# Two-block transformer layer on one core: the second layer's feed-forward part moved into the program of its attention

## The reference, cut to what matters

```python
ya = _dilated_attention(qa, ka, va)                     # width 512
yb = _mla(c_q, c_kv, k_r, ...)                          # width 512
y = concat([rmsnorm(ya, out_norm_a), rmsnorm(yb, out_norm_b)]) @ w_o
x = x + rmsnorm(y, norm_mix_post)
h = rmsnorm(x, norm_ffn_pre)
u = dwconv(h @ w_up, conv_w, conv_b)                    # 3 taps along the tokens, 2 x 2816 columns
g, v = u[..., :D_FF], u[..., D_FF:]                     # D_FF = 2816
y = (gelu(g, approximate=True) * v) @ w_down
x = x + rmsnorm(y, norm_ffn_post)
# rmsnorm(x, g) = x * rsqrt(mean(x*x) + EPS) * g
```

## Time and profile before

| | us |
|---|---|
| median of 3 runs | 2170.84 (2170.11 to 2176.09) |
| profiled execution, its own time | 2173.72 |
| its span, first to last instruction | 2171.1 |
| PE busy | 1936.4 (89%) |
| second attention's last output product ends | 1906.1 |
| first `downs` product starts | 1939.9 |
| the last unit's `downs` starts | 2150.9 |

### The profile page before, as it was taken

How to read it: one execution, slowest core, us unless ns; L and a number is a source line. 1 busy time by engine, 2 the same in 40 slices (tenths; PEclk the granted TensorE clock), 3 DMA queues, 4 the chain that set the end, 5 groups by cost and what they waited for, 6 DMA issues and landing times. The chain is left out here.

```text
span 2171.1 us, 24938 instructions
## 1 busy us (share of the span) xinstructions
PE 1936.4 (89%) x9338; PEld 1049.2 (48%) x9340; DVE 622.1 (29%) x1362; ACT 434.6 (20%) x855; POOL 67.3 (3%) x86
## 2 busy tenths in 40 slices
PE   5999797998989979999898888989989888979997
PEld 2436353886878543333333333233333245657774
DVE  2376346245520121111111111111111123442223
ACT  2122550326231011111111110111111022411011
POOL 1000310100000000000000000000000000000000
PEclk9999898798999989999999999999999999989998
DMA  9443336214374469999999999999999872034442
GB/s 348 144 167 137 131 98 145 94 55 143 93 282 164 161 248 418 418 418 417 417 417 418 418 417 419 418 419 418 416 418 417 336 267 78 1 118 153 162 148 87
DMA packets 150651, 566.73 MB, mean 261 GB/s; under 512 B 35872, under 2 KB 43808, under 8 KB 112736
## 3 DMA queue, kind: packets, MB, share of 16 engines
q1 hardware_dynamic: 150592, 565.92, 67.2%
HBM read 555.26 MB, written 10.62 MB: 261 GB/s over the span
## 5 line engine op out<-in xcount | busy, mean ns | idle before, releaser
L2006 PE MATMUL expert_gb<-expert_ring,hT 128*64 128x512 f32 x1024 | 270.4, 607 | 69.6 <-DMA expert_ring<-in_w_gu 68.1
L2006 PE MATMUL expert_lb<-expert_ring,hT 128*64 128x512 f32 x1024 | 262.8, 592 | 0.0
L1911 DVE TENSOR_SCALAR hT<-expert_gb 128x512 f32<-128x512 f32 x32 | 22.1, 692 | 717.0 <-PE expert_lb L2006 717.0
L2054 PE MATMUL expert_yb<-expert_ring,hT 128*64 128x512 f32 x512 | 222.7, 592 | 1.5 <-DMA expert_ring<-in_w_down 1.4
L2054 PE MATMUL expert_yb<-expert_ring,h2T 128*64 128x512 f32 x512 | 222.8, 592 | 0.0
L2006 PEld LDWEIGHTS expert_gb<-expert_ring,hT 128*64 128x64 f32 x1024 | 59.4, 135 | 250.2 <-DMA expert_ring<-in_w_gu 200.5
L446 PE MATMUL mix_in_pj<-hT,mix_in_pj_ring 128*128 128x512 f32 (+1 forms) x384 | 147.1, 542 | 4.0 <-DVE hT L567 4.0
L2006 PEld LDWEIGHTS expert_lb<-expert_ring,hT 128*64 128x64 f32 x1024 | 72.8, 137 | 147.0 <-issue 147.0
L2711 PE MATMUL ffn_pu<-ffn_hT,ffn_wu 128*128 128x256 f32 x640 | 141.4, 379 | 0.0
L2054 PEld LDWEIGHTS expert_yb<-expert_ring,hT 128*64 128x64 f32 x512 | 69.9, 137 | 143.3 <-issue 140.5
L2711 PEld LDWEIGHTS ffn_pu<-ffn_hT,ffn_wu 128*128 128x128 f32 x640 | 121.6, 190 | 25.1 <-issue 9.6
(11 more groups left out here) (474 smaller groups left out, 2288.1 us busy)
## 6 DMA issues: line engine op xcount, KB each, us to landing
expert_ring<-in_w_gu SPq DMA_DIRECT2D x256, 1024.0 KB, 19.7
expert_ring<-in_w_down SPq DMA_DIRECT2D x128, 1024.0 KB, 20.7
fill_w<-in_w_fill SPq DMA_DIRECT2D x48, 512.0 KB, 3.7
mix_in_wm<-in_w_mod SPq DMA_DIRECT2D x11, 2048.0 KB, 9.1
ffn_wu<-in_w_up_units SPq DMA_DIRECT2D x22, 1024.0 KB, 6.2
mix_in_pj_ring<-in_w_in_units SPq DMA_DIRECT2D x12, 1024.0 KB, 4.8
ffn_wd<-in_w_down SPq DMA_DIRECT2D x22, 512.0 KB, 3.4
expert_ring<-in_w_in SPq DMA_DIRECT2D x4, 2048.0 KB, 11.4
```

Of the source, the lines that this page charges most:

```text
L1911: v.tensor_scalar(glu, gb[j][:], LIMIT, None, ALU.min).then_inc(s_glu, 1)
L2006: m = pe.matmul(b[halves[h], :], xT[:, k, x], ring[:, z, c0 + 512 * h:c0 + 512 * h + 512], start=False, stop=(k == KT - 1))
L2054: m = pe.matmul(yb[h][halves[j], :], hidT[j][:, c, hh * SLOTS:(hh + 1) * SLOTS], ring[:, z, a * F + 512 * h:a * F + 512 * h + 512], start= ...
```

## The change

There is one stage now, `second_layer_stage`, with one program for each engine. What it does:

- **Buffers.** The first slots of `w_up` and `w_down` lie in the expert ring where the key bias and the dilated attention's `qz` and `ka` were; conv, Gelu and output tiles lie over `w_in`'s last part. The banks are shared: `pu` = 2, 3; `py` = 0, 1, 6, 7; `pt` = 4, 5.
- **SP.** The feed-forward gains and taps are asked for behind `w_o`, and the first two units of both weights once 8 score steps are done (`s_e` 8); the loop runs one pass less. The output leaves in four quarters.
- **Output product.** The pairs' order is (0,0), (1,0), (0,1), (1,1). Roots are an ACT root with scale and EPS as bias, then a DVE reciprocal.
- **Hand-over.** Both tiles' chains (join, root, finish, norm, transpose) are written interleaved. ACT copies the low half of each transposed tile, DVE the high half. `ups_half(0,0)` and `ups_half(1,0)` run before tile 1's transposes.
- **End.** The last `downs` closes the banks itself and signals after each tile; ACT squares each half tile from PSUM; DVE scales it from PSUM. The root's table is asked for right behind the Gelu loop (`warm`).

The core of the diff:

```diff
+                sp.wait_ge(s_e, 8)
+                for z in range(2):
+                    up_in(z, z)
+                for z in range(2):
+                    down_in(z, z * P)
+                with sp.Fori(0, FT // 2 - 1) as i:
+                    for z in range(2):
+                        sp.wait_ge(up[z], i + 1)
+                        up_in(z, i * 2 + (2 + z))
+                        sp.wait_ge(d_free[z], i + 1)
+                        down_in(z, i * (2 * P) + (2 + z) * P)
+                for q in range(4):
+                    t, c = q // 2, slice(512 * (q % 2), 512 * (q % 2) + 512)
+                    sp.wait_ge(s_zd, q + 1)
+                    sp.dma_start(out[0, t * P:(t + 1) * P, c], zo[:, t, c]).then_inc(s_out, 16)
...
                 pe.wait_ge(s_wo, 32)
+                turn_out(1, 0, pT[0])
                 multiply(0, 0, 0, bank[0])
                 multiply(0, 0, 1, bank[1])
-                turn_out(1, 0, pT[0])
                 turn_out(1, 1, pT[1])
+                multiply(1, 0, 0, bank[4])
+                multiply(1, 0, 1, bank[5])
                 multiply(0, 1, 0, bank[6])
                 multiply(0, 1, 1, bank[7])
-                multiply(1, 0, 0, bank[4])
-                multiply(1, 0, 1, bank[5])
...
+                pe.wait_ge(s_ze, 1)
+                pe.wait_ge(s_f, 4)
+                for b in py:
+                    pe.matmul(flat(b), zero[:, 0:P], zero[:], start=True, stop=False)
...
+                turn_x(0)
+                ups_half(0, 0)
+                ups_half(1, 0)
+                turn_x(1)
+                for z in range(2):
+                    ups_half(z, 1).then_inc(up[z], 1)
...
+                def root_of(src, c, ready, n, sem):
+                    act.wait_ge(*ready)
+                    act.activation(junk[:], src, ACT.Square, accum_out=stat[:, c:c + 1]).then_inc(s_ys, 1)
+                    act.wait_ge(s_ys, n)
+                    act.activation(rstd[:, c:c + 1], stat[:, c:c + 1], ACT.Sqrt, scale=1.0 / D, bias=C.eps[:]).then_inc(sem, 1)
...
+                parted(0)
+                root_of(yo[:, 0, :], 10, (s_yo, 2), 6, s_or)
+                parted(1)
+                root_of(X[:, 0, :], 12, (s_x2, 1), 7, s_xr)
+                low_x(0)
+                root_of(yo[:, 1, :], 11, (s_yo, 4), 8, s_or)
+                root_of(X[:, 1, :], 13, (s_x2, 2), 9, s_xr)
+                low_x(1)
...
+                act.activation(warm[:], C.eps[:], ACT.Sqrt)
                 for t in range(2):
+                    act.wait_ge(s_yd, t + 1)
+                    for h in range(2):
+                        q = 2 * t + h
+                        if q:
+                            act.wait_ge(s_zs, q)
+                        act.activation(junk[:, 0:512], flat(py[q]), ACT.Square, scale=1.0 / 32,
+                                       accum_out=stat[:, 14 + q:15 + q]).then_inc(s_zs, 1)
+                    act.wait_ge(s_zr, 2 * t + 1)
+                    act.activation(rstd[:, 14 + t:15 + t], stat[:, 14 + 2 * t:15 + 2 * t], ACT.Sqrt).then_inc(s_ra, 1)
...
+                join(0, 0)
+                join(0, 1)
+                finish(0)
+                join(1, 0)
+                normed(0)
+                join(1, 1)
+                high_x(0)
+                finish(1)
+                normed(1)
+                high_x(1)
...
+                    close(v.reciprocal(rstd[:, 14 + t:15 + t], rstd[:, 14 + t:15 + t]))
+                    for h in range(2):
+                        q, c = 2 * t + h, slice(512 * h, 512 * h + 512)
+                        link(v.scalar_tensor_tensor(zo[:, t, c], flat(py[q]), rstd[:, 14 + t:15 + t], gpost2[:, c],
+                                                    ALU.mult, ALU.mult))
+                        v.tensor_tensor(zo[:, t, c], X[:, t, c], zo[:, t, c], ALU.add).then_inc(s_zd, 1)
```

More of the change, by code:

```diff
@@ L2117, in attend_stage @@
         pr, prT = again(2, 2, L), again(2, 4, P)
+        hT2, xn2 = again(KT, L), S.x
         wukv = Cut(S.ob[:].rearrange("p k n -> p (k n)"))(2, 2 * WA)
@@ new lines, in ups_half @@
+                def ups_half(z, t):
+                    pe.wait_ge(u_in[z], 16)
+                    pe.wait_ge(s_l2, t + 1)
+                    pe.wait_ge(s_h2, t + 1)
+                    pe.wait_ge(s_yo, 4)
+                    for g in range(2):
+                        for k in range(KT):
+                            m = pe.matmul(pu[z][:, g, t * P:(t + 1) * P], wu[:, z, k, g * P:(g + 1) * P],
+                                          hT2[:, k, t * P:(t + 1) * P], start=(k == 0), stop=(k == KT - 1))
+                    return m
@@ new lines, in ups, with downs @@
+                def ups(z, landed):
+                    pe.wait_ge(u_in[z], landed)
+                    for g in range(2):
+                        for k in range(KT):
+                            m = pe.matmul(pu[z][:, g, :], wu[:, z, k, g * P:(g + 1) * P], hT2[:, k, :],
+                                          start=(k == 0), stop=(k == KT - 1))
+                    m.then_inc(up[z], 1)
+                def downs(z, n, last=False):
+                    pe.wait_ge(d_in[z], n * 16)
+                    pe.wait_ge(hidden[z], n)
+                    for t in range(2):
+                        for h in range(2):
+                            m = pe.matmul(flat(py[2 * t + h]), ac[:, z, t * P:(t + 1) * P], wd[:, z, 512 * h:512 * h + 512],
+                                          start=False, stop=last, skip_group_check=not last)
+                        if last:
+                            m.then_inc(s_yd, 1)
+                    if not last:
+                        m.then_inc(d_free[z], 1)
@@ L2328, in copy_turned @@
+                turn_x(0)
[4 more added lines that the diff above has]
+                    ups_half(z, 1).then_inc(up[z], 1)
+                with pe.Fori(0, FT // 2 - 1) as i:
+                    for z in range(2):
+                        downs(z, i + 1)
+                        ups(z, i * 16 + 32)
+                downs(0, FT // 2)
+                downs(1, FT // 2, True)
             def copy_turned(act, n):
@@ L2427, in _, with parted @@
                     square_out(1, t)
[L2428 to L2431, removed]
+                act.wait_ge(s_ys, 5)
+                act.activation(rstd[:, 6:10], stat[:, 6:10], ACT.Sqrt, scale=1.0 / WA, bias=C.eps[:]).then_inc(s_or, 1)
+                act.wait_ge(s_yr, 1)
+                def parted(t):
                     for h in range(2):
-                        act.wait_ge(s_po, 2 * t + h + 1)
+                        act.wait_ge(s_po, (1, 5)[t] + h)
@@ new lines, in low_x @@
+                def low_x(t):
+                    act.wait_ge(s_g2, 48)
+                    act.wait_ge(s_t2, 2 * t + 1)
+                    for k in range(4):
+                        m = act.activation(hT2[:, k, t * P:(t + 1) * P], bank[pt[0]][:, k, :], ACT.Copy, scale=gcol2[:, k:k + 1])
+                    m.then_inc(s_l2, 1)
+                parted(0)
+                root_of(yo[:, 0, :], 10, (s_yo, 2), 6, s_or)
+                parted(1)
+                root_of(X[:, 0, :], 12, (s_x2, 1), 7, s_xr)
@@ L2576, in _ @@
                     gain(1, t, pT[t])
[L2577 to L2580, removed]
                 v.wait_ge(s_or, 1)
[L2582 to L2592, removed]
+                v.reciprocal(rstd[:, 6:10], rstd[:, 6:10]).then_inc(s_yr, 1)
@@ new lines, in finish, with normed, high_x @@
+                    v.tensor_tensor(X[:, t, :], X[:, t, :], yo[:, t, :], ALU.add).then_inc(s_x2, 1)
+                def normed(t):
+                    v.wait_ge(s_xr, t + 1)
+                    last_norm(v.reciprocal(rstd[:, 12 + t:13 + t], rstd[:, 12 + t:13 + t]))
+                    v.tensor_scalar(xn2[:, t, :], X[:, t, :], rstd[:, 12 + t:13 + t], None, ALU.mult).then_inc(s_xn, 1)
+                def high_x(t):
+                    v.wait_ge(s_g2, 48)
+                    v.wait_ge(s_t2, 2 * t + 2)
+                    for k in range(4, 8):
+                        m = v.tensor_scalar(hT2[:, k, t * P:(t + 1) * P], bank[pt[1]][:, k - 4, :], gcol2[:, k:k + 1], None,
+                                            ALU.mult)
+                    m.then_inc(s_h2, 1)
```

218 lines of the change are left out of this document (58 added, 160 removed).

## The result

| | before | after |
|---|---|---|
| median | 2171.04 (4 runs, 2170.11 to 2176.09) | 2151.72 (4 runs, 2149.45 to 2157.18) |
| ratio | | 0.991, 95% interval 0.9893 to 0.9927 |
| span of the profiled execution | 2171.1 | 2150.9 |
| first seam: last output product to first `downs` | 33.8 | 20.8 |
| between: first to last unit's `downs` | 211.0 | 211.1 |

What follows compares the result with a forecast made beforehand. PE, busy 89% of the span, bounds the kernel, so only its idle or slow time at two seams can be won: 13.2 + 6.3 = 19.5 us, giving a median of 2151.3, range 2147 to 2158 for 8 in 10.

Steps and rivals of the forecast that it cites:

- first seam: Last output product to first `downs`: 33.8 us before, 20.6 forecast, so the loop starts 13.2 us earlier; bounds 10 and 15.8.
- The loop: Feed-forward `downs` and `ups` on PE alone, without waits: stays at 10.34 us a unit.
- The rests of PE: Before the first `downs`, PE waits about 1.3 us twice, for each tile's transposed copies.
- the spare time of the chains: Tile 0's and tile 1's norm chains on ACT and DVE are hidden behind PE, with 1.6 and 1.0 us to spare.
- The earlier pair: Output product in new order: part 1 of tile 0 is done one pair, 6.9 us, earlier.
- the attention's row: Profile row cited against a clock fall: in the attention PE idles 2.8 of 3.0 us at clock 1.00.
- The swing between the levels: Rival, 10%: short rests in the new seam drop the clock to 0.50, 2.0 us per spell; two give 2155.3.
- The second seam: Start of last `downs` to span's end: 20.2 us before, 14 forecast, a gain of 6.3; bounds 5 and 7.5.
- The store: Output's last piece at the end, 256 KB instead of 512: lands 0.3 us sooner; bounds 0 and 0.6.
- all of the hand-over between the programs: Barrier, table reload and second program's square of `X`, between attention and loop: counted inside the 33.8 us, no own terms.
- disturbance of the attention by the loads: Rival, 3%: 3 MB of early weight loads slow the attention's score steps, taking back 13 of 19.5 us; 2166.
- the 9.6 that it may take: Rival, 4%: in the loop `w_up` lands later than 9.6 us after its request, so phases wait; 2179 at 11.0.

Runs made afterwards that it cites:

- late_loads: The changed kernel, but the first two units of w_up and w_down asked for only once tile 1 of X is done: 2162.36 us, ratio to before 0.9951.
- seq_chain: The changed kernel with ACT's and DVE's chains written tile after tile and stage after stage, loads still early: 2161.61 us, ratio to before 0.9946.
- old_pairs: The changed kernel with the output product's pairs in the old order (0,0), (0,1), (1,0), (1,1): 2148.84 us, a single execution.
- after_again: The changed kernel unedited, measured once more beside another run on the same chip: 2153.49 us, ratio to before 0.9904.

## Why the prediction was right

- **The loop kept its time.** 211.1 us against 211.0.
- **The first seam**, forecast 20.6, is 20.8. The rests of PE are 1.49 each (forecast 1.3); the spare time of the chains, 1.7 and 1.3 us (forecast 1.6 and 1.0). `late_loads` shows that the load was PE's wait, and `seq_chain` that the early load alone would not have kept PE fed: the clock's share is in both.
- **The earlier pair counts for little.** The prediction gave the new order of the pairs as the ground for tile 0's early chain and took the chain as hidden. `old_pairs` puts a number on it: 0.2 us. In the changed kernel the fourth pair, which tile 1's join waits for in DVE's queue, sets when tile 0's norm comes.
- **The clock stayed** at 1.00 through two rests of 1.49 us, as the attention's row had it; it fell to 0.50 in the rests of 5.20 and 9.78 us in `seq_chain` and `late_loads`. The swing between the levels that the Trainium skill describes (TensorE: Matmul & The Clock Gate, section A second HAM failure mode) is not seen here.
- **The second seam**, forecast 14 from its start to the span's end, is 14.4. The work up to the last addition is right (10.5, forecast 10.6). The store was worth more than forecast, 0.6 instead of 0.3: 2.0 us to landing against 2.6. The formula of the Trainium skill (DMA: Bandwidth & Descriptors, section Anatomy of one DMA), which is for the GpSimd path, gives 0.6 for the halving as an estimate; its absolute times, 2.6 and 3.2, are longer than the trace's. The miss is a term that wasn't there: 0.9 us for clearing semaphores at the end. The prediction set all of the hand-over between the programs as gone; this part of it only moved.
- **Rivals.** No disturbance of the attention by the loads is seen above that part's own spread, and a `w_up` unit lands in 6.4 us in the median (6.2 before), far from the 9.6 that it may take.
- **The median** agrees with the forecast within 0.4 us, and that closeness is luck: 0.7 us too much was taken for the seams (19.5 against 18.8, with 13.2 and 6.3 against 13.0 and 5.8), the spread of the part ahead of them is larger than that, and the same kernel measured again, `after_again`, has a median of 2153.49, 2.2 us above the forecast.

## What to carry to other kernels

When a stage begins with a load, ask for it in the stage before, and then look at what PE waits for next: here half of what the first seam gave was the order of PE's, DVE's and ACT's steps. Price a long rest of PE with the clock that it brings down; two remedies for one long rest don't add up. When programs are joined, find the row for what closed the old one: it may only have moved to the end.

## What the runs showed of the hardware that was not expected

- Clearing a stage's semaphores takes POOL 132 ns for 18 and 477 ns for 81 of them, in one instruction, and each closing costs a barrier too; two in a row take 1.5 us (2149.4 to 2150.9).
- GpSimd's addition of 128 x 512 numbers takes 1.25 us with DVE at work, and two DVE operations beside it are stretched: 0.15 to 0.79 and 0.69 to 1.20 us. DVE's scaling from PSUM is not.
- A table load that follows a square directly started 0.02 us behind its read-out, with no drain between them.
- The same 1 MB load lands in 4.76 us when no other was asked for just ahead of it (`late_loads`), and in 7.43 behind three others.
